# A gated unit moved into an attention loop, a third bank for its scores, and an output projection taken up group by group

## The chip, the cores and the metric

The kernel runs on one core of one Trainium2 chip. The metric is the device time of one execution in microseconds; of three executions of the kernel before the median is 3381.57 us.

The engines are named as the profile names them: PE is the matrix engine (TensorE), ACT the scalar engine, DVE the vector engine, POOL GpSimd, SP the engine that issues most transfers. Each works through its own list of instructions in order and stops at a semaphore that is not there yet.

## What is computed

Two layers, each with a mixer, a cross-attention to a memory, and a large expert stage. The change lies in the mixer alone. Cut to what matters, the mixer is:

```python
c_q, c_kv, k_r, u_ssm, q_sb, k_sb, v_sb = split_columns(x @ w_in, IN_WIDTHS)
y_mla = chunk_causal_softmax_attention(q, k, v)        # latent attention, 6 heads of 64
y = jax.nn.gelu(scan_of(u_ssm))                        # state space part, 384 wide
y_ssm = y * jax.nn.sigmoid(y @ w_glu + b_glu)          # the gated unit
y_sb = stick_breaking_attention(q_sb, k_sb, v_sb)      # 4 heads of 64
y = jnp.concatenate([group_rms(y_mla), group_rms(y_ssm), group_rms(y_sb)], axis=-1) * g_mix
mix = y @ w_out                                        # the output projection, 1024 x 1024
```

The sequence has 512 positions, the model is 1024 wide. The program approximates gelu by tanh both before and after the change.

## The kernel before, in words

Everything is held transposed: features on the 128 partitions, the 512 positions along the free axis. y has eight such tiles: 0 to 2 are the latent attention, 3 to 5 the state space part (they lie in u), 6 and 7 the stick-breaking attention. The order of every engine is written out by hand in the function mixer, with one inner function per engine; semaphores tie them together. Nothing reorders it.

**The loop of the latent attention.** It has 24 turns, i = 0 to 23: six heads with four query blocks each (block b = i mod 4 sees b + 1 blocks of 128 keys). A turn's work goes round four stations. PE makes the scores (mla_s, line 898, one matmul 128 to 512 wide), DVE takes their largest value (mla_max), ACT takes the exponential into prob (line 1107), DVE scales it by the sum (mla_scale), PE transposes it, one 128x128 matrix per key block (mla_t, line 907), ACT copies the result out of PSUM into probT (mla_copy, line 1525), and PE multiplies it with the values (mla_o, line 921). prob and probT have two slots each, and the scores two banks, 4 and 5. Two waits matter below. ACT's exponential of turn i writes the slot that the transposes of i - 2 read, so it waits for them:

```python
            if i >= 2:
                act.wait_ge(m.mla_tr, i - 1)
```

And mla_o(i) waits until ACT has copied turn i (`pe.wait_ge(m.mla_pt, i + 1)`). In program turn i, PE issues mla_s(i + 1), mla_t(i - 1), mla_o(i - 2); ACT issues the exponential of i, then the copy of i - 2, and after the last block of every second head one copy of the result (mla_out, line 1531).

Into the first twelve turns DVE has the last two units of the state space scan strewn, six pieces each; PE has ssm_in and ssm_out for them (lines 829, 844, 847). After ssm_skip(2) on DVE, SP sends the scan's result out to DRAM and back in another layout, into u.

**The tail.** After the loop ACT squares y tiles 6, 7, 0, 1, 2 (line 1121), PE sums the squares over the partitions with a matrix of ones (squares, line 951), and ACT makes 1/rms of the two attention groups with a Ln and an Exp (rms, lines 1127 and 1129). ACT loads the table for gelu, applies it to u (line 1144), and loads the one for sigmoid. PE makes the nine products of the gated unit (line 960), ACT the sigmoid (line 1151), DVE the product, then come the squares and the rms of the third group. Each y tile is scaled (norm, line 1463), split into a high half in 16 bits by ACT (high, line 1133) and the rest by DVE (low, line 1471), for the matmuls take three 16-bit products in place of one in 32 bits. The state space tiles are read and written with a stride there (in_time).

**The output projection** has eight tiles of 128 output features. Each tile takes 8 x 3 = 24 matmuls 512 wide (project, lines 127 to 129). Tiles 0 and 1 are begun with the five y tiles of the attention groups and finished with the last three, tiles 2 to 7 follow, in two banks by turns. Weight tiles come through a ring of four (RING): DMA into wf, high half by ACT, low by DVE, then used; a slot is free when tile_used counts its last use. Behind the projection PE goes on with the memory's key tiles (256 wide, the first at line 127 with work as its input), the layer norm's sums between them.

## Time and profile before

| | us |
|---|---|
| median of three executions | 3381.57 (3372.29, 3381.57, 9482.11) |
| the profiled execution | 3381.33 |
| its span, first to last instruction | 3379.6 |
| PE busy in the span | 3208.7 (95%) |
| DVE, ACT busy | 2717.6, 1411.2 |
| layer 1: first score of the loop to last transposes | 176.59 to 227.90 |
| layer 1: last transposes to the end of the output projection | 227.90 to 297.51 |
| layer 2: the same end points | 1907.82 and 1978.86 |

Times within an execution are microseconds from the first instruction. The clock column of the stage table is PE's granted clock as a share of 2.4 GHz: 0.50 is the lower of its two levels, 1.2 GHz. A row of the time line gives the start, the duration, and, in brackets, how long the engine had stood idle and what released it. Durations of neighbouring rows on PE overlap, since matmuls are pipelined: the step from one start to the next is the price in a full stream. A matmul in 32 bits appears as two.

### The profile page before, as it was taken

The numbers are of one execution on the slowest core, as the hardware profiler recorded it, in microseconds if no ns is written. First come the engines' busy times: TensorE is split into PE (matmuls) and PEld (weight loads), VectorE is DVE, ScalarE is ACT, GpSimd is POOL, SyncE is SP. The second block draws the span as 40 slices with busy tenths as digits, with TensorE's granted clock in tenths as the row PEclk, the third lists the DMA queues.
The fourth block names the chain that finished last, engine by engine and source line by source line (L and its number), as shares of the span: only waits on it lengthen the run. The fifth ranks groups of instructions, "written<-read, shape, count | busy, mean of one in ns | idle before, by whom it ended". The sixth has DMA issues, their size and how long they took to land. (4 is left out here: it accounts for less than half of the span.)

```text
span 3379.6 us, 58399 instructions
## 1 busy us (share of the span) xinstructions
PE 3208.7 (95%) x20362; PEld 1966.0 (58%) x20362; DVE 2717.6 (80%) x5214; ACT 1411.2 (42%) x2117; POOL 1005.3 (30%) x754
## 2 busy tenths in 40 slices
PE   7989999999999899999799899999999998999996
PEld 3645665565666566666445465655656665666663
DVE  6866458898999788888877563688989997888887
ACT  4454443343444333333444543433444443333333
POOL 2400000332404344444324000003424144444442
PEclk9999999999999999999899999999999999999998
DMA  5103222889898999999551032338898989999994
GB/s 195 48 13 106 94 94 96 293 279 365 277 340 288 402 389 386 397 397 366 192 161 35 13 131 69 107 101 301 271 379 278 329 302 403 388 386 399 390 371 181
DMA packets 395484, 846.02 MB, mean 250 GB/s; under 512 B 34368, under 2 KB 239168, under 8 KB 394560
## 3 DMA queue, kind: packets, MB, share of 16 engines
q1 hardware_dynamic: 321024, 570.38, 47.6%
q0 software_dynamic: 73728, 268.47, 22.2%
q10 hardware_dynamic: 576, 5.37, 0.4%
q8 instruction: 64, 1.05, 0.1%
q14 instruction: 92, 0.75, 0.1%
HBM read 733.99 MB, written 110.10 MB: 250 GB/s over the span
## 5 line engine op out<-in xcount | busy, mean ns | idle before, releaser
L98 ACT ACTIVATE wh<-wf 128x1024 f16<-128x1024 f32 x656 | 690.8, 1053 | 947.9 <-PE ps L2132 545.8
L127 PE MATMUL ps<-xh,wh 128*128 128x384 f16 (+2 forms) x3008 | 1011.7, 336 | 78.2 <-DVEq L1273 37.4
L129 PE MATMUL ps<-xh,wl 128*128 128x384 f16 (+2 forms) x3008 | 1011.1, 336 | 0.0
L128 PE MATMUL ps<-xl,wh 128*128 128x384 f16 (+2 forms) x3008 | 1010.9, 336 | 0.0
L104 DVE SCALAR_TENSOR_TENSOR wl<-wf,wh 128x1024 f16<-128x1024 f32 x656 | 801.4, 1222 | 222.0 <-ACT wh L98 203.5
L2130 PE MATMUL ps<-work,wh 128*128 128x384 f16 x2048 | 668.9, 327 | 8.0 <-DVE work L2462 6.1
L2132 PE MATMUL ps<-work,wl 128*128 128x384 f16 x2048 | 669.2, 327 | 0.0
L2131 PE MATMUL ps<-work,wh 128*128 128x384 f16 x2048 | 669.1, 327 | 0.0
L2247 POOL DMA_INDIRECT xT<-urows,small x256 | 390.4, 1525 | 904.9 <-DVE xT L2330 650.4
L2256 POOL DMA_INDIRECT work<-experts,small x256 | 451.0, 1762 | 559.7 <-DVE work L2471 533.7
L127 PEld LDWEIGHTS ps<-xh,wh 128*128 128x128 f16 x3008 | 296.3, 99 | 303.3 <-DVEq L1273 38.4
L129 PEld LDWEIGHTS ps<-xh,wl 128*128 128x128 f16 x3008 | 296.1, 98 | 222.3 <-issue 5.3
L128 PEld LDWEIGHTS ps<-xl,wh 128*128 128x128 f16 x3008 | 296.2, 98 | 212.1 <-issue 6.4
L2471 DVE SCALAR_TENSOR_TENSOR work<-work,small 128x1024 f32<-128x1024 f32 x256 | 328.7, 1284 | 97.2 <-DVE work L2462 96.5
L2330 DVE SCALAR_TENSOR_TENSOR xT<-xT,work 128x1024 f32<-128x1024 f32 x256 | 308.2, 1219 | 72.6 <-DMA xT<-urows,small 71.6
L2130 PEld LDWEIGHTS ps<-work,wh 128*128 128x128 f16 x2048 | 200.8, 98 | 141.8 <-issue 8.0
L2132 PEld LDWEIGHTS ps<-work,wl 128*128 128x128 f16 x2048 | 200.7, 98 | 133.0 <-issue 1.0
L2131 PEld LDWEIGHTS ps<-work,wh 128*128 128x128 f16 x2048 | 200.8, 98 | 132.2 <-issue 1.3
L2189 ACT ACTIVATE work<-ps 128x384 f32<-128x384 f32 x192 | 93.7, 488 | 334.5 <-PE ps L129 334.4
L2457 DVE TENSOR_TENSOR work<-work 128x384 f32<-128x384 f32 x256 | 141.0, 551 | 0.5 <-DMA work<-gates 0.5
L2462 DVE SCALAR_TENSOR_TENSOR work<-work 128x384 f16<-128x384 f32 x256 | 141.0, 551 | 0.0
L220 POOL TENSOR_SCALAR xT<-xT,small 128x512 f32<-128x512 f32 x16 | 27.2, 1701 | 368.7 <-ACT xh L199 368.7
(414 smaller groups left out, 3746.7 us busy)
## 6 DMA issues: line engine op xcount, KB each, us to landing
wf<-experts SPq DMA_DIRECT2D x512, 512.0 KB, 6.9
wf<-proj SPq DMA_DIRECT2D x144, 512.0 KB, 3.4
gates<-work SPq DMA_DIRECT2D x96, 512.0 KB, 8.1
work<-hid SPq DMA_DIRECT2D x256, 192.0 KB, 4.8
work<-gates SPq DMA_DIRECT2D x256, 192.0 KB, 6.3
hid<-work SPq DMA_DIRECT2D x192, 192.0 KB, 5.3
hid<-small SPq DMA_DIRECT2D x64, 192.0 KB, 5.3
xsave<-xT ACTq DMA_DIRECT2D x2, 2048.0 KB, 6.5
```

The source lines that it names most:

```text
L98: m.nc.scalar.activation(m.wh[:, slot, :], m.wf[:, k, :], ACT.Copy, scale=WS).then_inc(m.high_done, 1)
L104: m.nc.vector.scalar_tensor_tensor(m.wl[:, slot, :], m.wf[:, k, :], WS, m.wh[:, slot, :], ALU.mult, ALU.subtract).then_inc(m.split_done, 1)
L127: m.nc.tensor.matmul(out, wh[:, k, :], xh[:, k, 0:n], start=(k == order[0]), stop=False)
L128: m.nc.tensor.matmul(out, wh[:, k, :], xl[:, k, 0:n], start=False, stop=False)
L129: last = m.nc.tensor.matmul(out, wl[:, k, :], xh[:, k, 0:n], start=False, stop=(k == order[-1]))
L2130: MM(out, m.wh[:, k, c], ph[:, k, :], start=first, stop=False)
L2131: MM(out, m.wh[:, k, c], pl[:, k, :], start=False, stop=False)
L2132: done = MM(out, m.wl[:, k, c], ph[:, k, :], start=False, stop=last)
L2247: pool.indirect_dma_start(urow[:, i % GR, :], None, a.urows, bass.IndirectOffsetOnAxis(ap=uidx[:, i:i + 1], axis=0))\
L2256: pool.indirect_dma_start(vrow[:, i % GR, :], None, rows, bass.IndirectOffsetOnAxis(ap=vidx[:, i:i + 1], axis=0))\
L2330: STT(row, row, 1.0, xtok, ALU.mult, ALU.mult, accum_out=hd[:, i:i + 1]).then_inc(m.dots, 1)
L2471: STT(acc, row, wd[:, bass.ds(i, 1)], acc, ALU.mult, ALU.add).then_inc(m.added, 1)
```

## The change

- **Scores run two turns ahead.** mla_s(i + 2) stands where mla_s(i + 1) stood, in three banks (4, 5, 1). ssm_in of the units from 4 on keeps to bank 0 and waits for one more unit.
- **mla_o(i - 2) is issued before mla_t(i - 1).** Before, it was the other way round.
- **The gated unit goes into the loop.** gelu and sigmoid are written with tanh: ACT squares u, DVE makes u(1 + c u^2), ACT takes the tanh, DVE makes (tanh + 1) u, twice gelu; the sigmoid likewise is half of 1 + tanh of half its argument. The factor 4 that this leaves is taken back by SSM_PART = 0.25. Turns 15 to 18 hold the gelu, turns 18 to 23 the nine products on PE, turns 18 to 20 four squares, turns 21, 22 and the end the gate. One table set holds Exp, Tanh, Square and Copy; it is loaded once ahead of the loop, and the one for Ln behind it. Before, three were loaded in the tail.
- **The output projection goes group by group.** Four tiles in four banks take up y tiles 6 and 7, then 3, 4, 5, then 0, 1, 2; then tiles 4 to 7 follow whole. The sums of four squares are made right behind the last transposes, the other four behind the first part.
- ssm_skip(2) comes one turn earlier (13).

```diff
+Y_ORDER = [6, 7, 3, 4, 5, 0, 1, 2]
+SSM_TILES = (3, 4, 5)
+SSM_PART = 0.25
+SQUARES = [(6, 1, 0, 2), (7, 1, 1, 2), (0, 0, 0, 3), (1, 0, 1, 3), (3, 2, 0, 3), (4, 2, 1, 3), (5, 2, 2, 3), (2, 0, 2, 3)]
+GROUP_BANK = {1: (4, 0), 0: (5, 1), 2: (1, 2)}
+GLU_I = 15
+GLU_AT = {18: ((0, 0), (0, 1)), 19: ((1, 0), (1, 1)), 20: ((0, 2),), 21: ((1, 2),), 22: ((2, 0), (2, 1)), 23: ((2, 2),)}
+GELU_CUBE = 0.044715
+GELU_SCALE = (2 / math.pi) ** 0.5
+EXP_TANH = "exp_and_others"
...
+    def score_bank(i):
+
+        return B[(4, 5, 1)[i % 3]]
+
+    def glu_bank(j):
+
+        return B[(0, 2)[j % 2]]
+
+    def out_bank(f):
+
+        return B[(0, 2, 3, 6)[f % RING]]
...
-            if i >= 2:
-                pe.wait_ge(m.mla_e, i - 1)
+            if i >= 3:
+                pe.wait_ge(m.mla_e, i - 2)
             n = P * (b + 1)
-            MM(B[4 + i % 2][:, 0:n], qh[:, h, b * P:n], kh[:, h, 0:n], start=True, stop=True)\
+            MM(score_bank(i)[:, 0:n], qh[:, h, b * P:n], kh[:, h, 0:n], start=True, stop=True)\
...
+        def glu_product(j, c):
+            if (j, c) == (0, 0):
+                pe.wait_ge(m.glu_in, 16)
+            if j == 0:
+                pe.wait_ge(m.gelu_done, (3, 4, 6)[c])
+            if (j, c) == (2, 0):
+                pe.wait_ge(m.glu_sig, 7)
+            last = MM(glu_bank(j), glu[:, c, j * P:(j + 1) * P], u[:, c, :], start=(c == 0), stop=(c == 2))
+            if c == 2:
+                last.then_inc(m.glu_mm, 1)
+
         for i in range(len(iters)):
-            if i and i + 1 < len(iters):
-                mla_s(i + 1)
+            if i + 2 < len(iters):
+                mla_s(i + 2)
             if i % PIECES == 0 and i and BH + i // PIECES - 1 < UNITS:
                 ssm_out(BH + i // PIECES - 1)
             if i == 1:
                 pe.wait_ge(m.ssm_y, 2)
+            if i >= 2:
+                mla_o(i - 2)
             if i >= 1:
                 mla_t(i - 1)
-            if i >= 2:
-                mla_o(i - 2)
...
+            for j, c in GLU_AT.get(i, ()):
+                glu_product(j, c)
         mla_t(len(iters) - 1)
+
+        def squares(i):
+            g, c, n = SQUARES[i][1:]
+            if c == 0:
+                pe.wait_ge(m.mla_e, len(iters) - 2 + GROUP_BANK[g][1])
+            pe.wait_ge(m.grp_sq, i + 1)
+            MM(B[GROUP_BANK[g][0]], m.ones[:, :], sqs[:, i % 4, :], start=(c == 0), stop=(c == n - 1))\
+                .then_inc(m.grp_sum, 1)
+
+        for i in range(4):
+            squares(i)
         mla_o(len(iters) - 2)
         mla_o(len(iters) - 1)
 
-        def squares(i, g, c, n):
-            pe.wait_ge(m.grp_sq, i + 1)
-            MM(B[4 + g], m.ones[:, :], sqs[:, i % 4, :], start=(c == 0), stop=(c == n - 1))\
-                .then_inc(m.grp_sum, 1)
-
-        for i, x in enumerate([(1, c, 2) for c in range(2)] + [(0, c, 3) for c in range(3)]):
-            squares(i, *x)
-        pe.wait_ge(m.glu_in, 16)
-        pe.wait_ge(m.gelu_done, 3)
-        for j in range(3):
...
-        for c in range(3):
-            squares(5 + c, 2, c, 3)
-        order = [6, 7, 0, 1, 2, 3, 4, 5]
-        pe.wait_ge(m.yl_done, 5)
-        pe.wait_ge(m.glu_sig, 3)
-        for f in range(2):
+        def projected_part(k0, k1):
+            pe.wait_ge(m.yl_done, k1)
+            for f in range(RING):
+                n = N_IN + f
+                if k0 == 0:
+                    wait_tile(m, pe, n // RING, n % RING)
+                last = project(m, out_bank(f), n % RING, m.xh, m.xl, SEQ, Y_ORDER, slice(k0, k1))
+                if k1 == KT:
+                    last.then_inc(m.tile_used, 1)
+
+        pe.wait_ge(m.glu_sig, 9)
+        pe.wait_ge(m.mla_pt, len(iters))
+        projected_part(0, 2)
+        for i in range(4, KT):
+            squares(i)
+        projected_part(2, 5)
+        projected_part(5, KT)
+        for f in range(RING, N_OUT):
             n = N_IN + f
             wait_tile(m, pe, n // RING, n % RING)
...
+            pe.wait_ge(m.ln_mix.res_added, f - RING + 1)
+            project(m, out_bank(f), n % RING, m.xh, m.xl, SEQ).then_inc(m.tile_used, 1)
...
+        def glu_square(j):
+            act.wait_ge(m.ssm_y, GROUPS)
+            act.wait_ge(m.moved_back, 16 * STRIDE * (GROUPS + j + 1))
+            AF(sig[:, j, :], u[:, j, :], ACT.Square, scale=GELU_CUBE ** 0.5).then_inc(m.glu_sig, 1)
+
+        def glu_tanh(j):
+            act.wait_ge(m.gelu_done, (1, 2, 5)[j])
+            AF(sig[:, j, :], sig[:, j, :], ACT.Tanh, scale=GELU_SCALE).then_inc(m.glu_sig, 1)
+
+        def glu_gate(j):
+            act.wait_ge(m.glu_mm, j + 1)
+            AF(sig[:, j, :], glu_bank(j), ACT.Tanh, scale=0.25, bias=half_glu[:, j:j + 1]).then_inc(m.glu_sig, 1)
+
+        def square(i):
+            f = SQUARES[i][0]
+            if i >= 4:
+                act.wait_ge(m.grp_sum, i - 3)
+            AF(sqs[:, i % 4, :], y[f], ACT.Square, scale=SSM_PART if f in SSM_TILES else 1.0).then_inc(m.grp_sq, 1)
+
+        act.preload_act_table_set(EXP_TANH)
...
+            if i == GLU_I:
+                glu_square(0)
+                glu_square(1)
+            if i == GLU_I + 1:
+                glu_tanh(0)
+                glu_tanh(1)
+            if i == GLU_I + 2:
+                glu_square(2)
+            if i == GLU_I + 3:
+                glu_tanh(2)
+                act.wait_ge(m.sb_y, 2)
+                square(0)
+            if i == GLU_I + 4:
+                square(1)
+                act.wait_ge(m.mla_y, 2)
+                square(2)
+            if i == GLU_I + 5:
+                square(3)
+            if i == GLU_I + 6:
+                glu_gate(0)
+            if i == GLU_I + 7:
+                glu_gate(1)
         mla_copy(m, act, len(iters) - 2, iters, probT, B)
         mla_copy(m, act, len(iters) - 1, iters, probT, B)
-        mla_out(m, act, len(iters) - 1, iters, y, B)
...
+        glu_gate(2)
+        act.preload_act_table_set(LOG_EXP)
...
+        rms(0, 1, 2, BH * BD)
+        mla_out(m, act, len(iters) - 1, iters, y, B)
+        act.wait_ge(m.tile_used, N_IN + RING)
+        for i in range(2):
+            high(i)
+        for i in range(4, 7):
+            act.wait_ge(m.gelu_done, i + 3)
+            square(i)
         act.wait_ge(m.mla_y, 3)
-        for i in range(5):
-            square(i)
-        rms(0, 1, 2, BH * BD)
-        rms(1, 0, 5, MH * MV)
-        act.preload_act_table(ACT.Gelu_apprx_tanh)
-        for j in range(3):
-            act.wait_ge(m.moved_back, 16 * STRIDE * (GROUPS + j + 1))
...
-        for j in range(3):
...
+        def gelu_argument(j):
+            dve.wait_ge(m.glu_sig, (1, 2, 5)[j])
+            STT(sig[:, j, :], sig[:, j, :], 1.0, u[:, j, :], ALU.add, ALU.mult).then_inc(m.gelu_done, 1)
+
+        def gelu_twice(j):
+            dve.wait_ge(m.glu_sig, (3, 4, 6)[j])
+            STT(u[:, j, :], sig[:, j, :], 1.0, u[:, j, :], ALU.add, ALU.mult).then_inc(m.gelu_done, 1)
+
+        def gated(j):
+            dve.wait_ge(m.glu_sig, 7 + j)
+            dve.wait_ge(m.glu_mm, 3)
+            STT(u[:, j, :], sig[:, j, :], 1.0, u[:, j, :], ALU.add, ALU.mult).then_inc(m.gelu_done, 1)
+
+        TS(half_glu, par[:, PAR["b_glu"]], 0.5, None, ALU.mult)
         for i in range(len(iters)):
             mla_max(i)
             if i == 1:
@@ -1438,8 +1521,18 @@
                 mla_scale(i - 1)
             n, piece = BH + i // PIECES, i % PIECES
             if n >= UNITS:
-                if (n, piece) == (UNITS, 2):
+                if (n, piece) == (UNITS, 1):
                     ssm_skip(2)
+                if i == GLU_I:
+                    gelu_argument(0)
+                    gelu_argument(1)
+                if i == GLU_I + 1:
+                    gelu_twice(0)
+                    gelu_twice(1)
+                if i == GLU_I + 2:
+                    gelu_argument(2)
+                if i == GLU_I + 3:
+                    gelu_twice(2)
...
+        for j in range(3):
+            gated(j)
         norm(1, 1, (0, 1))
-        norm(0, 2, (2, 3, 4))
-        for i in range(5):
+        for i in range(2):
             low(i)
-        for j in range(3):
-            dve.wait_ge(m.glu_sig, j + 1)
-            dve.wait_ge(m.glu_mm, 3)
-            TT(u[:, j, :], u[:, j, :], sig[:, j, :], ALU.mult).then_inc(m.glu_done, 1)
-        dve.wait_ge(m.grp_sq, 8)
-        norm(2, 3, (5, 6, 7))
+        norm(2, 2, (2, 3, 4))
+        for i in range(2, 5):
+            low(i)
+        norm(0, 3, (5, 6, 7))
...
```

The order on PE within a turn, before (scores are line 898, transposes 907, products with the values 921). These are program turns 8 and 9: scores of 9, transposes of 7, products of 6, then scores of 10, transposes of 8, products of 7:

```order
L898 MATMUL ps<-work 128x256 [waits mla_e]
L907 MATMUL ps<-ident,work 128x128 [waits mla_pt,mla_p]
L907 MATMUL ps<-ident,work 128x128 x3
L921 MATMUL ps<-work 64x128 [waits mla_pt]
L921 MATMUL ps<-work 64x128 x2
L898 MATMUL ps<-work 128x384 [waits mla_e]
L907 MATMUL ps<-ident,work 128x128 [waits mla_pt,mla_p]
L921 MATMUL ps<-work 64x128 [waits mla_pt]
L921 MATMUL ps<-work 64x128 x3
```

And now, program turns 7 and 8 (scores are line 925, transposes 934, products with the values 948): scores of 9, products of 5, transposes of 6, then scores of 10, products of 6, transposes of 7:

```order
L925 MATMUL ps<-work 128x256 [waits mla_e]
L948 MATMUL ps<-work 64x128 [waits mla_pt]
L948 MATMUL ps<-work 64x128
L934 MATMUL ps<-ident,work 128x128 [waits mla_pt,mla_p]
L934 MATMUL ps<-ident,work 128x128 x2
L925 MATMUL ps<-work 128x384 [waits mla_e]
L948 MATMUL ps<-work 64x128 [waits mla_pt]
L948 MATMUL ps<-work 64x128 x2
L934 MATMUL ps<-ident,work 128x128 [waits mla_pt,mla_p]
L934 MATMUL ps<-ident,work 128x128 x3
```

The products with the values now stand behind the scores and ahead of the transposes; before, the transposes stood between.

The end of the loop on PE before (951 the sums of squares, 960 the gated unit, 127 the projection):

```order
L921 MATMUL ps<-work 64x128 [waits mla_pt]
L921 MATMUL ps<-work 64x128 x3
L951 MATMUL ps<-work,ones 128x512 [waits grp_sq] x5
L960 MATMUL ps<-work 128x512 [waits gelu_done,glu_in]
L960 MATMUL ps<-work 128x512 x8
L951 MATMUL ps<-work,ones 128x512 [waits grp_sq] x3
L127 MATMUL ps<-xh,wh 128x512 [waits split_done,glu_sig,yl_done]
L128 MATMUL ps<-xl,wh 128x512
```

And now (966 the gated unit, 992 the sums of squares):

```order
L966 MATMUL ps<-work 128x512
L934 MATMUL ps<-ident,work 128x128 [waits mla_pt,mla_p]
L934 MATMUL ps<-ident,work 128x128 x3
L992 MATMUL ps<-work,ones 128x512 [waits grp_sq,mla_e]
L992 MATMUL ps<-work,ones 128x512 [waits grp_sq]
L992 MATMUL ps<-work,ones 128x512 [waits grp_sq,mla_e]
L992 MATMUL ps<-work,ones 128x512 [waits grp_sq]
L948 MATMUL ps<-work 64x128 [waits mla_pt]
L948 MATMUL ps<-work 64x128 x2
L948 MATMUL ps<-work 64x128 [waits mla_pt]
L948 MATMUL ps<-work 64x128 x3
L127 MATMUL ps<-xh,wh 128x512 [waits yl_done,split_done,mla_pt,glu_sig]
```

The nine products are gone from this place, four sums stand ahead of the last products with the values, and the projection follows at once, with its waits.

ACT in turns 15 to 17 now (1169 the exponential, 1617 the copy, 1145 the square and 1149 the tanh of the gelu):

```order
L1169 ACTIVATE work,small<-ps,small 128x512 [waits mla_tr,mla_nm]
L1617 ACTIVATE work<-ps 128x256 [waits mla_av,mla_tr]
L1145 ACTIVATE sq<-work 128x512 [waits moved_back,ssm_y] x2
L1169 ACTIVATE work,small<-ps,small 128x128 [waits mla_tr,mla_nm]
L1617 ACTIVATE work<-ps 128x384 [waits mla_av,mla_tr]
L1149 ACTIVATE sq<-sq 128x512 [waits gelu_done] x2
L1169 ACTIVATE work,small<-ps,small 128x256 [waits mla_tr,mla_nm]
L1617 ACTIVATE work<-ps 128x512 [waits mla_av,mla_tr]
L1145 ACTIVATE sq<-work 128x512 [waits moved_back,ssm_y]
L1169 ACTIVATE work,small<-ps,small 128x384 [waits mla_tr,mla_nm]
```

The tanh of turn 16 waits for DVE, which waits for the square of turn 15; neither was in the loop before.

## Rows read from the trace of the kernel before

**Rows 1.** Busy time by stage: length, busy us of each engine, PE's clock, DMA.

```profile
170.00:176.00 6.00, 3.36 (x19) 2.17 (x18) 4.17 (x10) 1.24 (x1) 3.21 (x5) 1.00 0.00 0
242.00:244.00 2.00, 2.00 (x4) 0.68 (x3) 1.36 (x3) 2.00 (x4) 0.00 (x0) 0.50 0.00 0
```

**Rows 2.** Time line of PE, one head of the loop, layer 1.

```profile
211.56 0.55 PE L907 MATMUL ps<-ident,work 128*128 128x128 f32 x3 [0.50 <-DVE work L1431]
...
212.70 0.70 PE L898 MATMUL ps<-work 128*128 128x256 f32 x2
213.24 0.60 PE L907 MATMUL ps<-ident,work 128*128 128x128 f32 x4
...
214.57 0.91 PE L898 MATMUL ps<-work 128*128 128x384 f32 x2
215.31 0.27 PE L907 MATMUL ps<-ident,work 128*128 128x128 f32 x1
...
216.53 1.12 PE L898 MATMUL ps<-work 128*128 128x512 f32 x2
217.50 0.38 PE L907 MATMUL ps<-ident,work 128*128 128x128 f32 x2
...
218.17 0.49 PE L898 MATMUL ps<-work 128*128 128x128 f32 x2
```

**Rows 3.** Time line of PE, program turns 5 and 6 of layer 1.

```profile
190.36 1.09 PE L921 MATMUL ps<-work 128*64 128x128 f32 x8 [0.36 <-ACT work L1525]
191.38 1.12 PE L898 MATMUL ps<-work 128*128 128x512 f32 x2
...
193.68 0.38 PE L907 MATMUL ps<-ident,work 128*128 128x128 f32 x2
```

**Rows 4.** Time line of ACT, turns 2 to 7 of layer 1.

```profile
183.26 0.58 ACT L1107 ACTIVATE work<-ps,small 128x384 f32<-128x384 f32 x1 [2.31 <-DVE small L1425]
...
189.26 0.48 ACT L1107 ACTIVATE work<-ps,small 128x256 f32<-128x256 f32 x1 [1.60 <-DVE small L1425]
...
189.72 0.59 ACT L1525 ACTIVATE work<-ps 128x512 f32<-128x512 f32 x1
...
194.16 0.69 ACT L1107 ACTIVATE work<-ps,small 128x512 f32<-128x512 f32 x1 [2.34 <-PE ps L907]
```

**Rows 5.** Time line of PE, the tail of layer 1.

```profile
227.90 0.66 PE L907 MATMUL ps<-ident,work 128*128 128x128 f32 x4
...
231.74 4.56 PE L951 MATMUL ps<-work,ones 128*128 128x512 f32 x10 [1.41 <-ACT work L1121]
240.81 9.66 PE L960 MATMUL ps<-work 128*128 128x512 f32 x18 [4.51 <-ACT work L1144]
253.18 2.84 PE L951 MATMUL ps<-work,ones 128*128 128x512 f32 x6 [2.72 <-ACT work L1121]
255.86 0.38 PE L127 MATMUL ps<-xh,wh 128*128 128x512 f16 x1
```

**Rows 6.** Time line of PE, where the memory's tiles begin, layer 1.

```profile
297.51 0.27 PE L127 MATMUL ps<-work,wh 128*128 128x256 f16 x1
```

**Rows 7.** Time line of PE, the last three squares of layer 2.

```profile
1933.00 4.36 PE L951 MATMUL ps<-work,ones 128*128 128x512 f32 x6 [2.72 <-ACT work L1121]
```

**Rows 8.** Time line of ACT, the tail of layer 1.

```profile
240.68 1.28 ACT L1145 ACT_TABLE_LOAD   x1
241.97 2.71 ACT L1133 ACTIVATE xh<-work 128x512 f16<-128x512 f32 x5
...
256.06 0.69 ACT L1127 ACTIVATE work<-ps,eps 128x512 f32<-128x512 f32 x1 [1.90 <-PE ps L951]
...
258.31 3.09 ACT L1133 ACTIVATE xh<-work 128x512 f16<-128x512 f32 x3 [0.90 <-DVE work L1463]
```

**Rows 9.** Time line of DVE, the tail of layer 1.

```profile
257.53 2.08 DVE L1463 SCALAR_TENSOR_TENSOR work<-work,small 128x512 f32<-128x512 f32 x3 [5.06 <-ACT work L1129]
259.52 2.96 DVE L1471 SCALAR_TENSOR_TENSOR xl<-work,xh 128x512 f16<-128x512 f32 x3
```

More of the change, by code:

```diff
@@ L668, in mixer @@
     mx, nmx, rsum, rinv = (small.take([2]) for _ in range(4))
+    half_glu = small.take([3])
     y = [qh[:, 2 * j, :] for j in range(3)] + [u[:, j, :] for j in range(3)] + [qsb[:, j, :] for j in range(2)]
@@ L828, in ssm_in @@
                     st = 2 * n + i
-                    last = MM(cols(B[n % 2], 2 * z + i), in_weights(z, st), inputs_of(st), start=True, stop=True)
+                    last = MM(cols(in_bank(n), 2 * z + i), in_weights(z, st), inputs_of(st), start=True, stop=True)
             last.then_inc(m.ssm_bu, 1)
@@ L958, in tensor @@
-        for j in range(3):
-            for c in range(3):
-                last = MM(B[j], glu[:, c, j * P:(j + 1) * P], u[:, c, :], start=(c == 0), stop=(c == 2))
-            last.then_inc(m.glu_mm, 1)
-        for c in range(3):
-            squares(5 + c, 2, c, 3)
-        order = [6, 7, 0, 1, 2, 3, 4, 5]
-        pe.wait_ge(m.yl_done, 5)
-        pe.wait_ge(m.glu_sig, 3)
-        for f in range(2):
+        def projected_part(k0, k1):
[7 more added lines that the diff above has]
+                    last.then_inc(m.tile_used, 1)
@@ L968, in tensor @@
+        pe.wait_ge(m.glu_sig, 9)
[6 more added lines that the diff above has]
+        for f in range(RING, N_OUT):
             n = N_IN + f
             wait_tile(m, pe, n // RING, n % RING)
-            project(m, B[f], n % RING, m.xh, m.xl, SEQ, order, slice(0, 5))
-        pe.wait_ge(m.yl_done, KT)
-        for f in range(2):
-            project(m, B[f], (N_IN + f) % RING, m.xh, m.xl, SEQ, order, slice(5, KT))\
-                .then_inc(m.tile_used, 1)
@@ L1106, in scalar @@
                 act.wait_ge(m.sb_o, BH)
-            AF(prob[:, i % 2, 0:n], B[4 + i % 2][:, 0:n], ACT.Exp, scale=MLA_SCALE,
+            AF(prob[:, i % 2, 0:n], score_bank(i)[:, 0:n], ACT.Exp, scale=MLA_SCALE,
                bias=nmx[:, i % 2:i % 2 + 1], accum_out=rsum[:, i % 2:i % 2 + 1]).then_inc(m.mla_e, 1)
@@ L1131, in high @@
         def high(i):
+            f = Y_ORDER[i]
             act.wait_ge(m.y_norm, i + 1)
-            AF(*in_time(m.xh[:, order[i], :], y[order[i]], i >= 5), ACT.Copy, scale=XS).then_inc(m.yh_done, 1)
-        act.wait_ge(m.sb_y, 2)
-        act.wait_ge(m.mla_y, 3)
-        for i in range(5):
-            square(i)
-        rms(0, 1, 2, BH * BD)
-        rms(1, 0, 5, MH * MV)
-        act.preload_act_table(ACT.Gelu_apprx_tanh)
-        for j in range(3):
-            act.wait_ge(m.moved_back, 16 * STRIDE * (GROUPS + j + 1))
-            AF(u[:, j, :], u[:, j, :], ACT.Gelu_apprx_tanh).then_inc(m.gelu_done, 1)
-        act.preload_act_table(ACT.Sigmoid)
-        act.wait_ge(m.tile_used, N_IN + RING)
-        for i in range(5):
-            high(i)
-        for j in range(3):
-            act.wait_ge(m.glu_mm, j + 1)
-            AF(sig[:, j, :], B[j], ACT.Sigmoid, bias=par[:, PAR["b_glu"]][:, j:j + 1]).then_inc(m.glu_sig, 1)
-        act.preload_act_table_set(LOG_EXP)
-        for j in range(3):
-            act.wait_ge(m.glu_done, j + 1)
-            square(5 + j)
-        rms(2, 2, 8, SG * SC)
-        for i in range(5, KT):
+            AF(*in_time(m.xh[:, f, :], y[f], f in SSM_TILES), ACT.Copy,
+               scale=XS * SSM_PART if f in SSM_TILES else XS).then_inc(m.yh_done, 1)
+        rms(0, 1, 2, BH * BD)
[6 more added lines that the diff above has]
+            square(i)
+        act.wait_ge(m.mla_y, 3)
+        square(7)
+        rms(1, 2, 7, SG * SC)
+        rms(2, 0, 8, MH * MV)
+        for i in range(2, KT):
             high(i)
@@ L1421, in mla_max @@
             dve.wait_ge(m.mla_sc, i + 1)
-            step(nc.vector.reduce_max(mx[:, k:k + 1], B[4 + k][:, 0:n], AX.X))
+            step(nc.vector.reduce_max(mx[:, k:k + 1], score_bank(i)[:, 0:n], AX.X))
             if i >= 2:
@@ L1455, in vector @@
         mla_scale(len(iters) - 1)
-        order = [6, 7, 0, 1, 2, 3, 4, 5]
         def norm(k, need, tiles):
@@ L1461, in norm @@
             for i in tiles:
-                f = order[i]
+                f = Y_ORDER[i]
                 STT(y[f], y[f], par[:, PAR["g_mix"]][:, f:f + 1], grs[:, k, :], ALU.mult, ALU.mult)\
```

39 lines of the change are left out of this document (14 added, 25 removed).

## The prediction, made before the change was run

> **What bounds the kernel now.** I read the profile from the outside in. The page first: PE, the matrix engine, is busy for 95% of the span, and nearly all the rest of the program, the experts above all, is untouched. Whatever the change does, it does in the mixer of each layer, between the first score of the latent attention and the end of the output projection, two stretches of some 121 us. PE's time line comes next, for PE is the engine that starts the following stage, and everything behind the mixer hangs on its data: a microsecond won or lost there goes through to the end at face value. What counts is therefore PE's idle time and PE's clock in the two stretches.
>
> In the loop, the time line of one head shows PE nearly full. From the start of a turn's transposes to the next scores, transposes and products with the values take 1.14, 1.33, 1.22 and 0.67 us, together **4.36** a head; the scores take 0.54, 0.74 and 0.97 for 256, 384 and 512 columns, by the same spacing 0.33 for 128, together 2.58 [rows 2]. PE is thus busy 6.94 us a head, and the only pause of that head is 0.50.
>
> In the tail, from the last transposes at 227.90 to the memory's first tile at 297.51, 69.6 us pass in layer 1. PE pauses 1.41, 4.51 and 2.72 us there [rows 5, 6]. After the pause of 4.51 the granted clock is 0.50 [rows 1], and the nine products of the gated unit take 9.66 us. Five squares of the same width take 4.56 at full clock, 0.88 each without the overlap at the end, so nine cost 7.9 and the low clock costs **1.7**. After the pause of 2.72 the three squares take 2.84 in layer 1 and 4.36 in layer 2 [rows 5, 7]: there the clock fell in one of two cases. Layer 2's tail is 71.1 by that.
>
> **The loop: the order of transposes and values.** This is the part on which my forecast rests. ACT's exponential of turn i waits for the transposes of i - 2, then ACT copies these transposes out, then PE can make the products of i - 2. Before, PE had the transposes of i - 1 to issue between, so ACT worked while PE did. Now the products of i - 2 stand ahead of the transposes of i - 1. Only the scores of i + 2 cover ACT's two instructions, and the next transposes, which the next exponential waits for, come after. PE and ACT take turns in a ring: exponential, copy, values, transposes, exponential.
>
> ACT's share: exponentials of 256 and 512 columns take 0.48 and 0.69, one of 384 takes 0.58, so 0.37 for 128 and 2.12 for four. The copy of 512 takes 0.59; with the same steps four take 1.72. The handover is 0.05 from the copy's end (189.72 + 0.59) to PE's start at 190.36, and from PE to ACT 0.10 (193.68 + 0.38 to 194.16) plus about 0.07 of the transposes' tail that runs beyond their step: 0.2 a turn [rows 3, 4]. A head is 2.12 + 1.72 + 0.8 + 4.36 = **9.0 us**, where PE's own work is 6.94.
>
> Two ahead instead of one helps the scores, which then are never late, but they were not what held a full PE. I start where DVE still sets the pace in both versions, at the exponential of turn 2 at 183.26 [rows 4]. Turns 2 and 3 take 1.7 + 2.4, five heads 45.0, less the first handover: 48.9. ssm_out comes twice, 1.34 each (191.38 + 0.97 to 193.68) [rows 3]; what of it is not covered by the gap in the ring is 0.6 and 1.0. The last transposes would start at 183.26 + 50.5 = 233.8 instead of 227.90: **+5.9**.
>
> The other moves in the loop: ssm_in a turn later and in one bank costs nothing, since DVE has read the unit before long before and the gap in the ring hides it. The table load ahead of the loop, 1.28 [rows 8], delays the first exponential, hidden behind DVE's scan and skip work; uncovered it would be 1.3. ssm_skip one turn earlier is 0.
>
> **The gated unit in the loop.** Nine products at full clock: 7.9. Those in turns 18 to 23 fill gaps in the ring, 0.3 or 0.7 a turn, 3.2 in all. Against that stands a chain between ACT and DVE in turns 15 to 18. In turn 15 the two arguments on DVE wait for ACT's square (0.6) and take 0.7 each [rows 9]; the largest value of turn 16 (0.4 with its scaling) is queued behind them, so its exponential starts 2.4 after the copy of turn 13 and not 1.3: 1.1 lost. The same way I get 0.9 in turn 17, 0.5 in 18 and 0.7 in 19 with ACT's tanh, square and result copy in front: 3.2. Bounds: 0, if DVE runs far enough ahead, to 6, twice as much, if each of the four waits also holds the turn behind it. I take 3.2; with the filled gaps it cancels, and the unit costs **7.9**. The DMA of the scan's result has four turns, 9 us, before it is needed, and costs 0. The loop thus ends 5.9 + 7.9 = **13.8 us later**.
>
> **The tail now.** PE: last transposes 0.6, four squares 3.5, two products with values 1.8 = 5.9. ACT meanwhile: copy 0.6, gate 0.7, table 1.28, Ln and Exp 0.7 each, done before PE is. Then a result copy 0.6, two high halves 0.6 each, the last low half 0.7: PE starts the first part at 8.4, after a **pause of 2.5**. A matmul of the projection is (297.51 - 255.86) / 192 = 0.217 [rows 5, 6]. First part, 24 of them: 5.2. Four squares: 3.5, PE free at 17.1. The third of them, at 16.2, releases Ln and Exp of the state space group, Ln and Exp of the latent group stand behind on ACT (2.8 in all), then three strided high halves, 3.09, then the last strided low half, 1.0 [rows 8, 9]: 23.1, a **pause of 6.0**. Then 72 matmuls 15.6 and four whole tiles 20.8: 59.5. The weight tiles of the ring come free 1.9 us apart instead of 5.2, but the first is needed 5.9 after its slot is free, and ACT and DVE need about 3 for it: 0.
>
> The clock: the pause of 6.0 is longer than the 4.51 that cost 1.7, so 1.7 again. The pause of 2.5 is nearest to the 2.72 that cost 0 and 1.5: I take 0.8, ends 0 and 1.5. Tail 62.0, against 69.6 and 71.1: **7.6 and 9.1 won**.
>
> A switch of ACT's table: its load ends at 241.96 and the next ACTIVATE starts at 241.97 [rows 8]; nothing stands between. The Trainium skill (ScalarE: Activation LUTs, What ACT_TABLE_LOAD costs) adds a drain to each load, about 2.66 us for the switch; by that, ACT would finish in the tail at about the time of PE's last products, and the sum would be 0.2 us higher. I go by the row.
>
> **The sum.** 13.8 - 7.6 = 6.2 in layer 1, 13.8 - 9.1 = 4.7 in layer 2: 10.9, say 11. The profiled execution took 3381.3 (span 3379.6, 1.7 around it), which is also the median shown: **3392**. The nine products are moved, not removed; what the tail wins is mostly their time.
>
> **Rivals.**
> - *The ring has slack, the scores two ahead do their work.* Then the copy is not what ends last, PE runs at 6.94 a head, and the loop loses its pauses, like the 0.50 at transposes that waited for DVE [rows 2]; I put eight such as gone, 4 us. Loop -4 + 7.9 + 3.2 = +7.1, less 7.6 and 9.1: -2.5, so 3379; without the chain's 3.2, 3372. For it: the scores are early. Against it: the waits in the code leave no way round. 17%.
> - *The chain and the clock cost their upper bounds.* Another 3 us for the gelu and 0.7 for the clock in each layer: 3400; with DVE late for whole turns, 3405. 10%.
> - *Slower beyond doubt: the clock falls in the loop.* With a pause in every turn PE's busy share there drops from 0.93 to about 0.77. If the clock went to its lower level for the whole loop, a head would take 4.4 more plus scores no longer covered, and the nine products 7.9 more, some 43 us a layer: 3480. For half the loop, 3435. It decides where short pauses alone are enough. Against it: a stage of 6 us with PE busy for 3.36 has clock 1.00 [rows 1]. The Trainium skill (TensorE: Matmul & The Clock Gate, A second HAM failure mode) tells of a kernel that cycled through PSUM banks and, with small pauses between its groups, lost its clock again and again; that is this rival. 3%, half of it over 2%.
> - *It does not do what it says.* Nothing reorders the lists, and ACT's holds two table loads where three were. I give it nothing.
>
> **Chances and range.** The forecast's own case has 70%: 3384 to 3400. The 17% of slack spread from 3372 to 3383. The range leaves out its lower third and the top: **3375 to 3402**. 2% of the time is 68 us, about what a measurement of this kernel tells from no change; only the clock reaches it. Faster 0.01, same 0.97, slower 0.02.
>
> **What would show it.** In the profile after, a head of the loop in turns 4 to 15 takes 9.0 us, PE's idle time in the loop is ended by ACT's copy (before: by DVE), and ACT's idle time ahead of the exponential by PE's transposes. The last transposes of layer 1 start near 242. The nine products take 0.9 each. In the tail, pauses of about 2.5 and 6, the low clock after the second. The forecast is wrong if PE does not wait for the copy in the loop, or if the loop's last transposes start before 238.

## The result, and the profile after

The changed kernel takes **3389.29 us** (3387.14 to 3389.84, 5 runs), the kernel before 3380.96 (3372.29 to 9482.11, 5 runs); the ratio is 1.0034, 95% interval 1.0019 to 1.0048. One slow run of the kernel before, of 9482.11 us, is left out of the ratio. In a second comparison, with 12 and 17 runs, the ratio was 1.0040 (1.0027 to 1.0052). By the two ratios it is slower by 11.5 and 13.5 us; the medians differ by 8.3 and 15.0. The prediction said +11 and 3392, with a range of 3375 to 3402.

Stages of both layers, from the profiled executions (loop: exponential of turn 2 to the start of the last transposes; tail: from there to the memory's first tile; mixer part: first transposes to the memory's first tile):

| us | loop 1 | tail 1 | mixer part 1 | loop 2 | tail 2 | mixer part 2 |
|---|---|---|---|---|---|---|
| before | 44.64 | 69.61 | 115.59 | 44.65 | 71.04 | 117.02 |
| predicted | 58.4 | 62.0 | | 58.4 | 62.0 | |
| after | 58.39 | 63.46 | 123.19 | 61.26 | 61.77 | 124.36 |
| after, second profile | 58.39 | 63.46 | 123.18 | 58.38 | 63.47 | 123.19 |

PE's time line in the loop after, turns 7 to 9 of layer 1 (948 values, 934 transposes, 925 scores), answers to [rows 2]:

```profile
196.59 0.65 PE L948 MATMUL ps<-work 128*64 128x128 f32 x4 [0.77 <-ACT work L1617]
197.18 0.55 PE L934 MATMUL ps<-ident,work 128*128 128x128 f32 x3
197.56 0.81 PE L925 MATMUL ps<-work 128*128 128x384 f32 x2
198.71 0.87 PE L948 MATMUL ps<-work 128*64 128x128 f32 x6 [0.34 <-ACT work L1617]
199.51 0.66 PE L934 MATMUL ps<-ident,work 128*128 128x128 f32 x4
200.00 1.02 PE L925 MATMUL ps<-work 128*128 128x512 f32 x2
201.37 1.09 PE L948 MATMUL ps<-work 128*64 128x128 f32 x8 [0.34 <-ACT work L1617]
```

In these turns every group of products with the values has a pause in front that ACT's copy ends (where state space work or a product of the gated unit stands in between, there is none); before, one pause in a head stood in front of the transposes and was DVE's. ACT's time line of the same place (1169 exponential, 1617 copy), answering to [rows 4]:

```profile
197.82 0.37 ACT L1169 ACTIVATE work<-ps,small 128x128 f32<-128x128 f32 x1 [1.28 <-PE ps L934]
...
198.18 0.48 ACT L1617 ACTIVATE work<-ps 128x384 f32<-128x384 f32 x1
...
202.82 0.58 ACT L1169 ACTIVATE work<-ps,small 128x384 f32<-128x384 f32 x1 [1.50 <-PE ps L934]
...
203.39 0.27 ACT L1617 ACTIVATE work<-ps 128x128 f32<-128x128 f32 x1
```

Each exponential begins when PE's transposes are done, the copy follows at once, and ACT then stands idle until the next transposes. The two engines take turns. Without state space work or a result copy, the steps between the starts of PE's products are 2.12 and 2.66 (196.59, 198.71, 201.37) and, a head later, 2.33 and 2.01 (211.97, 214.30, 216.31): 9.12 us a head put together from the two, for 9.0 forecast. The product of turn 12 is the row of 214.30; it is used again below:

```profile
214.30 0.43 PE L948 MATMUL ps<-work 128*64 128x128 f32 x2 [0.77 <-ACT work L1617]
```

Who ended PE's idle time in the whole loop of layer 1, after and then before (total, times, longest):

```profile
PE ps L948 <- ACT work L1617: 9.0, 12, 1.7
PE ps L948 <- ACT work L1623: 3.1, 2, 1.8
```

```profile
PE ps L907 <- DVE work L1431: 3.4, 5, 0.9
PE ps L921 <- ACT work L1525: 0.4, 1, 0.4
```

In turns 15 to 18 the pauses are longer. DVE (1504 argument, 1491 largest value, 1494 its scaling, 1508 twice the gelu) and ACT (1145 square, 1169 exponential):

```profile
216.80 1.29 DVE L1504 SCALAR_TENSOR_TENSOR sq<-sq,work 128x512 f32<-128x512 f32 x2 [2.07 <-ACT sq L1145]
218.01 0.28 DVE L1491 TENSOR_REDUCE small<-ps 128x1 f32<-128x128 f32 x1
218.33 0.15 DVE L1494 TENSOR_SCALAR small<-small 128x1 f32<-128x1 f32 x1
...
219.91 1.29 DVE L1508 SCALAR_TENSOR_TENSOR work<-sq,work 128x512 f32<-128x512 f32 x2 [0.83 <-ACT sq L1149]
```

```profile
216.14 1.15 ACT L1145 ACTIVATE sq<-work 128x512 f32<-128x512 f32 x2
218.52 0.37 ACT L1169 ACTIVATE work<-ps,small 128x128 f32<-128x128 f32 x1 [1.23 <-DVE small L1494]
...
221.76 0.47 ACT L1169 ACTIVATE work<-ps,small 128x256 f32<-128x256 f32 x1 [1.36 <-DVE small L1494]
```

DVE stands idle 2.07 us for ACT's square, with the largest value of turn 16 queued behind, and the exponential of turn 16 waits for that; the same once more in turn 17.

PE's tail after, answering to [rows 5, 6] (992 squares, 127 projection, work,wh the memory's tile):

```profile
242.38 0.60 PE L934 MATMUL ps<-ident,work 128*128 128x128 f32 x4
242.82 3.60 PE L992 MATMUL ps<-work,ones 128*128 128x512 f32 x8
246.35 1.74 PE L948 MATMUL ps<-work 128*64 128x128 f32 x14
```

```profile
250.83 0.38 PE L127 MATMUL ps<-xh,wh 128*128 128x512 f16 x1 [2.74 <-DVE xl L1563]
...
257.69 3.60 PE L992 MATMUL ps<-work,ones 128*128 128x512 f32 x8
267.08 0.61 PE L127 MATMUL ps<-xh,wh 128*128 128x512 f16 x1 [5.79 <-DVE xl L1563]
...
305.84 0.27 PE L127 MATMUL ps<-work,wh 128*128 128x256 f16 x1
```

Pauses of 2.74 and 5.79 us, for 2.5 and 6.0 forecast. The clock (columns: window, length, busy time and count of PE, weight loads, DVE, ACT and POOL, the granted clock, DMA share, GB/s; the windows are the first part, the second part, and two places in the loop of layer 2):

```profile
252.00:258.00 6.00, 6.00 (x21) 2.50 (x20) 0.00 (x0) 0.00 (x0) 0.00 (x0) 0.74 0.01 3
266.00:268.00 2.00, 0.92 (x3) 0.37 (x4) 2.00 (x4) 0.28 (x1) 0.00 (x0) 0.50 0.00 0
270.00:272.00 2.00, 2.00 (x6) 0.76 (x5) 0.81 (x2) 0.00 (x0) 0.00 (x0) 0.50 0.00 0
...
1866.00:1870.00 4.00, 3.51 (x15) 2.84 (x15) 3.83 (x14) 1.49 (x6) 0.00 (x0) 0.57 0.24 70
1910.50:1914.00 3.50, 3.50 (x8) 1.50 (x7) 2.38 (x9) 2.09 (x5) 0.00 (x0) 0.51 0.02 5
```

After the first pause the clock is low for part of the stage at 252. Around the second it is at 0.50 from 265.3 to 272.1, 6.8 us of which PE works 5.1; after the pause of 4.51 before, it was low for 3.4 us. And it fell twice in the loop of layer 2, which explains 61.26 there against 58.39.

### The profile page after: what moved, and what is told of

The parts are those of the page before. It is cut to its first block and busy times, and to the rows that moved or that the text cites. A ratio compares the mean times of both kernels' runs of the same rounds, so it can differ in the third digit from the quotient of the medians.

```text
span 3385.4 us, 58423 instructions
## 1 busy us (share of the span) xinstructions
PE 3202.6 (95%) x20362; PEld 1962.7 (58%) x20362; DVE 2726.4 (81%) x5228; ACT 1412.8 (42%) x2121; POOL 996.5 (29%) x754
## 5 line engine op out<-in xcount | busy, mean ns | idle before, releaser
L2422 DVE SCALAR_TENSOR_TENSOR xT<-xT,work 128x1024 f32<-128x1024 f32 x256 | 308.7, 1222 | 60.4 <-DMA xT<-urows,small 59.5
```

Source lines behind the costliest of these rows:

```text
L2422: STT(row, row, 1.0, xtok, ALU.mult, ALU.mult, accum_out=hd[:, i:i + 1]).then_inc(m.dots, 1)
```

## The experiments

Every comparison shares one chip with runs of the kernel before. Times of the whole spread over some 14 us from run to run (the kernel before: 3371.31 to 3384.95 in the 29 runs of one comparison), the mixers' stages repeat within 0.02 us from profile to profile unless the clock differs; so the stages decide, and the whole is a check.

**The kernel before, again** (no edit).

> The kernel before, once more, for a second profile of it. It tells how far the same program drifts between two executions in the stages that the change does not touch. Theory A (the change costs about 19 us in the two mixers, and the stages between and behind them, which stream the experts' weights, came out about 13 us shorter in the profiled run of the changed kernel by chance): the mixers last as before within 0.5 us (layer 1 from the first transposes of the loop to the memory's first tile 115.6 us, layer 2 117.0), while the stretch from layer 1's mixer to layer 2's differs by several us from the 1564 us of before. Theory B (the shorter expert stages are an effect of the change): that stretch comes out as before within 1 us.

Mixer parts 115.61 and 117.03: the same. The stretch from layer 1's mixer to layer 2's took 1564.6 (first profile 1564.3), the rest behind 1400.9 (1400.7). Theory A's second half failed, B's held in this pair. In the ten profiles of the other kernels the stretch between the mixers took 1558.4 to 1562.2. More on it below.

**Transposes first.**

```diff
-            if i >= 2:
-                mla_o(i - 2)
             if i >= 1:
                 mla_t(i - 1)
+            if i >= 2:
+                mla_o(i - 2)
```

> The changed kernel with one pair of lines swapped back: the transposes of turn i - 1 are issued ahead of the products with the values of turn i - 2. Theory A (the ring between PE and ACT costs 5.9 us a layer): layer 1 from the exponential of turn 2 to the last transposes falls from 58.4 us to 52.5, a head without state space work takes 7.0 to 7.3 us and not 9.1, the whole 12 us less than the changed kernel, 3377. Rival (the gelu chain or DVE holds the loop anyway): the loop falls by less than 2 us, the whole by less than 4.

Loop 52.98 and 52.99, whole 3376.51 (ratio to before 1.000, 0.999 to 1.001). One pair of lines takes **5.4 us** from each loop and 12.1 us from the two mixer parts together (116.92 and 117.32); by the ratios, 1.0034 and 1.0040 against 1.000, it is 11 to 14 us of the whole. A head took 7.56 (transposes at 194.96 and 202.52), with a result copy and one pause for DVE in it, a little over the 7.0 to 7.3 expected. PE's waits in the loop of layer 1 are now:

```profile
PE ps L934 <- DVE work L1500: 4.4, 5, 1.3
PE ps L948 <- ACT work L1623: 0.5, 1, 0.5
PE ps L948 <- ACT work L1617: 0.4, 1, 0.4
```

The copy is gone from the list but for 0.4; DVE is back, 4.4. Of that, 2.7 (1.29, 0.53 and 0.85) stand in turns 16 to 18, and the other 1.7 in turns 2 and 11.

**The kernel before, values first.**

```diff
-            if i >= 1:
-                mla_t(i - 1)
             if i >= 2:
                 mla_o(i - 2)
+            if i >= 1:
+                mla_t(i - 1)
```

> The kernel before with only that pair of lines swapped: the products with the values of turn i - 2 ahead of the transposes of turn i - 1; scores stay one turn ahead. Theory A: the ring appears here too, a head takes 9.0 us and not 7.6, layer 1 from the exponential of turn 2 to the last transposes grows from 44.6 us to 50.5, the whole by 12 us to about 3390. Rival (the ring needs the scores two ahead, or the gated unit in the loop, to show): less than 2 us in the loop.

Loops 55.16 and 54.11, whole 3397.51 (ratio 1.0053, 1.0035 to 1.0071). The waits and the clock, of the loop of layer 1 and of 3.4 us in it:

```profile
PE ps L921 <- ACT work L1525: 10.8, 15, 1.2
PE ps L921 <- ACT work L1531: 1.4, 2, 0.7
```

```profile
183.00:237.00 54.00, 41.41 (x221) 26.86 (x220) 33.11 (x111) 21.50 (x68) 0.00 (x0) 0.94 0.05 16
206.60:210.00 3.40, 3.40 (x16) 3.21 (x14) 0.94 (x4) 0.84 (x3) 0.00 (x0) 0.51 0.00 0
```

The ring is there without gated unit and without scores further ahead. The loops grew by 10.5 and 9.5 us. The clock fell twice in the first loop and once in the second. Each fall can be priced by the same steps at full clock: 4.48 between the products of turns 9 and 10 where the changed kernel takes 3.05, so 1.4, and 2.75 and 3.07 late in the loop for 2.12 and 2.66, so 1.0. That leaves 8.1 us in both layers for the ring, where I had said 5.9. Rows of layer 2, at full clock, show where the miss lies (the row x7 holds the last seven transposes; the last four of them, where the loop ends, start at 1926.72):

```profile
1904.97 0.43 PE L921 MATMUL ps<-work 128*64 128x128 f32 x2
...
1911.75 1.09 PE L921 MATMUL ps<-work 128*64 128x128 f32 x8 [0.55 <-ACT work L1525]
1914.66 0.40 PE L921 MATMUL ps<-work 128*64 128x128 f32 x2 [0.71 <-ACT work L1531]
...
1926.34 0.98 PE L907 MATMUL ps<-ident,work 128*128 128x128 f32 x7
```

A turn whose copy is followed by a result copy (L1531) takes 2.91 and not 2.33: 0.6, twice, which the forecast of the ring left out. The first ssm_out costs 0.5 more than assumed, and a head 9.12 for 9.0, 0.6 over five heads.

**The kernel before, scores two ahead.**

```diff
-            if i and i + 1 < len(iters):
-                mla_s(i + 1)
+            if i + 2 < len(iters):
+                mla_s(i + 2)
```

with the banks (4, 5, 1) for the scores, bank 0 for the state space inputs, and ssm_in a turn later.

> The kernel before with only the scores two turns ahead in three banks (and, as that needs, the state space inputs in one bank, a turn later); transposes stay ahead of the products with the values. Theory A (scores ahead take away PE's waits for DVE): the pauses in the loop fall from 5.3 us to about 1.5, layer 1 from the exponential of turn 2 to the last transposes from 44.6 us to 41, the whole by 7 us. Rival (DVE sets the pace in the first half, so only the second half gains): 43, the whole 3 us less.

Loops 41.30 and 41.30, whole 3368.06 (ratio 0.9970, 0.9959 to 0.9981): 3.3 us a loop, and 7.5 in the medians of the whole. This part of the change, alone, makes the kernel faster. PE's waits in the loop:

```profile
PE ps L907 <- DVE work L1431: 1.7, 2, 1.3
PE ps L921 <- ACT work L1525: 0.4, 1, 0.4
```

**Filling the pauses of the tail.**

```diff
+        pe.wait_ge(m.mla_e, len(iters))
+        for _ in range(3):
+            MM(B[1][:, 0:3 * P], m.ones[:, :], glu[:, 0, :], start=True, stop=True)
         pe.wait_ge(m.glu_sig, 9)
...
         for i in range(4, KT):
             squares(i)
+        for _ in range(6):
+            MM(B[7], m.ones[:, :], sqs[:, 0, :], start=True, stop=True)
         projected_part(2, 5)
```

> The changed kernel with matmuls that compute nothing wanted put into PE's two pauses of the tail: three of 384 columns ahead of the projection's first part, six of 512 behind the last squares, the results unused. Theory A (the low clock after the pauses costs the projection 1.6 us and 2.9 us in layer 1, 2.9 us in layer 2): the clock stays at 1.00 to the end of the projection, the tail of layer 1 falls from 63.5 us to about 59.5, that of layer 2 from 61.8 to 59, the whole by 6 us. Rival (what costs is the pause, and its clock is repaid by the filling matmuls being late): the tail falls by less than 1 us or grows.

Tail 59.32 in both layers, whole 3381.22 (ratio 1.0011, 1.0001 to 1.0021). PE (1012 and 1019 are the filling):

```profile
251.13 2.20 PE L1012 MATMUL ps<-work,ones 128*128 128x384 f32 x6
253.93 0.38 PE L127 MATMUL ps<-xh,wh 128*128 128x512 f16 x1 [0.60 <-DVE xl L1568]
...
262.54 5.31 PE L1019 MATMUL ps<-work,ones 128*128 128x512 f32 x12
268.54 0.39 PE L127 MATMUL ps<-xh,wh 128*128 128x512 f16 x1 [0.69 <-DVE xl L1568]
```

The projection's parts begin 8.4 and 23.1 us behind the last transposes, as late as without filling in layer 2 of the first profile, where the first part ran at full clock; all of it now runs at full clock. The tail's low clock had cost 63.46 - 59.32 = **4.1 us** in layer 1, and 61.77 - 59.32 = 2.45 in layer 2, where only the second pause brought it. So it costs 1.65 behind the first pause and 2.45 behind the second; the 2.9 of my expectation is too high. The loop of layer 1 took 60.89 here, with the clock low in it for 6.8 us; that of layer 2 58.37.

**Two tiles instead of four, group by group.**

```diff
-            for f in range(RING):
+            for f in range(2):
...
-        for f in range(RING, N_OUT):
+        for f in range(2, N_OUT):
...
-            pe.wait_ge(m.ln_mix.res_added, f - RING + 1)
+            if f >= RING:
+                pe.wait_ge(m.ln_mix.res_added, f - RING + 1)
```

> The changed kernel with two tiles instead of four in the group by group part of the projection; tiles 2 to 7 follow whole, in the same four banks. Theory A (the pauses are set by ACT's and DVE's chain from the squares on, and four tiles only move that chain 2.6 us later): the first part takes 2.6 us less, the squares and all behind them come 2.6 us earlier, and the six tiles that follow take as much longer; tail of layer 1 63.5 us within 1, the whole the same within 3. Rival (four tiles cover what two leave open): a third pause of 1 to 3 us appears ahead of the last part, and the whole grows by 2 to 6 us.

Tails 63.17 and 63.01, loops 58.39 and 58.40, whole 3386.26 (ratio 1.0029, 1.0019 to 1.0040). Two tiles do as well as four: what is put ahead of the squares delays the chain behind them by as much.

**Transposes first, gelu spread, high halves earlier.** In DVE's list the parts of the gelu stand in turns 16 to 19 instead of 15 to 18; in the tail:

```diff
         rms(1, 2, 7, SG * SC)
+        for i in range(2, 5):
+            high(i)
         rms(2, 0, 8, MH * MV)
-        for i in range(2, KT):
+        for i in range(5, KT):
             high(i)
```

> The kernel with the transposes first again (3376.5), and two orders changed besides: DVE's part of the gelu one turn later in its list, so that it finds ACT's result ready, and in the tail the high halves of the state space tiles ahead of the Ln and Exp of the latent group. Theory A (the chain between ACT and DVE costs about 3 us in the loop, the order of Ln and Exp 1.3 in the tail): layer 1's loop falls from 53.0 us to 50, its tail from 62.6 to 61.3, the whole by 8 us to about 3368. Rival (the loop is held by something else, such as ACT's full list in turns 15 to 22): the loop falls by less than 1 us.

Loops 49.13 and 49.12, whole 3369.85 (ratio 0.9975, 0.9964 to 0.9985). The spread takes **3.85 us** from the loop. PE's waits there:

```profile
PE ps L934 <- DVE work L1502: 1.7, 2, 1.3
PE ps L948 <- ACT work L1625: 0.5, 1, 0.5
```

The tail did not move: 62.83 and 63.12 against 62.60 and 62.99. The pause fell from 5.79 to 5.52 only. ACT shows why:

```profile
255.00 0.63 ACT L1206 ACTIVATE work<-work 128x512 f32<-128x512 f32 x1
256.45 3.04 ACT L1211 ACTIVATE xh<-work 128x512 f16<-128x512 f32 x3 [0.82 <-DVE work L1557]
```

The high halves now wait 0.82 for DVE's scaling, which before went on beside the second Ln and Exp. My 1.3 had left that out.

**All together, with filling** (three and four matmuls).

> All together: transposes first, DVE's gelu a turn later, high halves ahead of the second Ln and Exp, and filling matmuls in both pauses (three of 384 columns, four of 512, results unused). Theory A: first transposes to the memory's first tile 109 us in both layers, where the kernel before takes 115.6 and 117.0 and the one with only the scores two ahead 113.7 and 112.3; the whole 14 us below before, 3362. Rival (the filling matmuls delay real work as much as the clock gives back): no better than without them.

Mixer parts 109.51 and 109.49; whole **3362.64** (ratio 0.9954, 0.9937 to 0.9971). It beats both kernels, by 15 us the one before.

**The changed kernel again** (no edit).

> The changed kernel once more, for a second profile and for a comparison on one chip with more runs. Theory A (the loop's clock falls now and then, since PE pauses in every turn): the loop of each layer takes 58.4 us, or up to 3 more where the clock falls in it; the two mixers together cost 13 to 17 us more than before (14.9 in the first profile); the whole 3388, 0.3 to 0.4% over before. Rival (the first profile's 61.3 us in layer 2 has another cause): both loops differ from 58.4 with the clock at 1.00 throughout.

Loops 58.39 and 58.38 with the clock at 1.00 in both, whole 3391.14 (ratio 1.0040). Mixer parts 13.8 us over before.

**Scores two ahead, with filling.** To the kernel with only the scores ahead:

```diff
         pe.wait_ge(m.glu_in, 16)
+        for _ in range(6):
+            MM(B[3][:, 0:3 * P], m.ones[:, :], glu[:, 0, :], start=True, stop=True)
         pe.wait_ge(m.gelu_done, 3)
...
+        for _ in range(3):
+            MM(B[3][:, 0:3 * P], m.ones[:, :], glu[:, 0, :], start=True, stop=True)
         for c in range(3):
             squares(5 + c, 2, c, 3)
```

> The kernel before with the scores two turns ahead, and filling matmuls of 384 columns in two pauses of its tail (six ahead of the gated unit's products, three ahead of the last squares, results unused). Theory A (the low clock costs this kernel 1.7 us at the products, and sometimes as much at the squares): the tail of both layers takes 67.9 us in place of 71.1 and 69.6, first transposes to the memory's first tile 110.5, the whole 5 us less than without the filling, 3363; the gated unit in the loop (109.5 with everything else mended) is then worth 1 us a layer. Rival (the moved gated unit is worth more): this kernel stays 3 us a layer or more behind it.

Tail 67.85 in both layers, mixer parts 110.49, whole 3362.89 (ratio 0.9953, 0.9935 to 0.9972). The nine products, 9.66 in [rows 5], at full clock:

```profile
240.44 7.99 PE L962 MATMUL ps<-work 128*128 128x512 f32 x18 [0.55 <-ACT work L1148]
```

Against 109.5 of the kernel with everything mended, the gated unit in the loop and the projection by groups are worth 1.0 us a layer by the stages. The whole does not tell the two apart (3362.64 and 3362.89, the intervals nearly the same).

## Why the prediction was right, point by point

**The loop.** Forecast +13.8, measured +13.75 in layer 1. The experiments take it apart; they nest, each differing from the next by one thing, but for the third line, where the gated unit and the tail's new form are added together:

| | loop, us | step | forecast |
|---|---|---|---|
| before | 44.64 | | |
| scores two ahead | 41.30 | -3.3 | to 41.3, PE's own work |
| gated unit, no waits in its chain | 49.13 | +7.8 | +7.9 |
| the chain between ACT and DVE | 52.98 | +3.85 | +3.2 |
| values ahead of transposes | 58.39 | +5.4 | +6.0 |

The forecast column is worked out of the prediction. Its loop without the gated unit was 50.5 long. The ring's gaps, 9.0 less 6.94 or 2.06 a head, are some 10.3 in the five heads; 1.1 of ssm_out's 2.7 was to lie in them, so the ring adds 9.2, and 41.3 are left for PE's own work. Products were to fill 3.2 of the gaps, so beside the gated unit the ring costs 6.0. The one step that made the forecast, that mla_o ahead of mla_t turns PE and ACT into a ring, is shown: by the waits after, by undoing it, and by doing it alone.

That the sum came out within 0.1 us was luck: two terms missed by about 1.5 us, one each way. No run has the ring with the scores two ahead and without the gated unit, but rows give an estimate of it. The changed kernel reaches the product of turn 12, still ahead of the gated unit, 30.3 us after the exponential of turn 2 (183.99 to 214.30). From there to the last transposes the kernel before with the values first takes 21.75 at full clock (1904.97 to 1926.72). Together that is a loop of some 52.1, so the ring costs some 7.4 where I had 5.9, for the reasons given at that run, and the gated unit some 6.3 where I had 7.9. By the same estimate the gaps are 10.8 and not 9.2, and the products fill some 5.4 of them and not 3.2 (10.8 less 5.4); the chain took 3.85 and not 3.2.

**The clock in the loop.** I gave it 3% as a rival with large prices, and nothing in the forecast. It does happen, rarely and at a small price: in the ten loops profiled with the values first it fell in four, and the loop grew by 2.5 (60.89 against 58.37) and 2.9 (61.26 against 58.38) where the same kernel's undisturbed loop stands beside it; in the 14 loops with the transposes first, never. One stage of 6 us at full clock with PE busy for 3.36 of it [rows 1] was too little evidence for a loop of 60.

**The tail.** Pauses 2.74 and 5.79 for 2.5 and 6.0; the chain of ACT and DVE was sized right. Without its clock the tail is 59.3 us (59.32 with filling), for 59.5 forecast. The clock was mis-sized: 1.65 and 2.45 us in layer 1 where I took 0.8 and 1.7. I had taken the cost of the pause of 4.51 for the longer one too, but PE worked at the low clock for 5.1 us after it, not 3.4. 62.0 became 63.46. That the group by group part wins nothing by having four tiles the prediction did not say, though its sum (59.5 whatever stands ahead of the squares) held it.

**The whole.** "Goes through to the end at face value" is not shown. In the first pair of profiles the mixers grew by 14.9 us and the span by 5.8; the stretches between and behind were 5.9 and 4.0 shorter. One piece of that is seen: both profiles of the kernel before have the clock low for 3.4 us in the layer norm behind the first mixer (at 306.0 and 307.6), those of the changed kernel have not. The rest lies in the expert stages. Between the mixers the clock records of the traces are low for 54.6 us in both profiles of the kernel before and for 44.4 in both of the changed kernel; PE's work at half speed for 10.2 us less would be up to 5.1 us, an estimate, of the 5.9 and of 5.0 in the second pair. What makes the clock differ there is not shown, and it is not all: with the values first alone it was low for 54.6 us too, and that stretch took 1562.2. By the ratios the whole grew by 11.5 and 13.5, near the mixers' 14.9 and 13.8; the profiled executions of the kernel before (3381.3, 3383.2) lie above most of its medians (3380.96, 3375.61, 3377.00 and 3376.17), those of the changed one (3387.14 and 3384.18) below its own (3389.29 and 3391.14). Whether more than such scatter is in it stays open. My +11 met the whole partly for this reason; the mixers alone were mis-sized by 3 to 4. In the second profile all of its 2.9 is the clock in the two tails, 1.5 in each; in the first the clock in the loop of layer 2 adds 2.9, and the tail there is 1.7 shorter.

**The rivals.** Slack in the ring is refuted. The chain at its upper bound is refuted: 3.85. The large price of the clock is refuted for the ten loops seen. That the scores ahead do work of their own is half borne out: alone they take 3.3 us from a loop, but in the ring some 0.7 is left of it (8.1 less the estimated 7.4).

## What to carry to other kernels

When two engines hand slots to each other, look at what one can still issue between the instruction the other waits for and the one that waits for it: one swapped pair of lines cost 5.4 us in 24 turns and hid a gain of 3.3 beside it. Work moved into a full loop costs its own length there, and pays only by what it frees at its old place, here 1 us a layer. Pauses of a few microseconds can be paid twice, once as idle time and once as a slower clock behind them: in the ten unfilled tails of the changed kernel and its variants the clock was low behind the longer pause (5.5 to 5.8 us) every time and behind the shorter (2.7) nine times. And a forecast that meets the number can still have two terms wrong: compare it stage by stage.

## What the runs showed that I had not expected

- Matmuls that compute nothing, put into pauses of 2.7 and 5.8 us, won 4.1 us of 63.5 in the changed tail of layer 1, and made both layers' tails equal to 0.01 us; without them the same tail varied from 61.77 to 63.47.
- The clock also differs from execution to execution ahead of the loop, where nothing was changed (from 135 to 182 us its mean was 1.00 in one profile of the changed kernel and 0.93 in the other): the first transposes start at 181.4 to 188.9 us in the twelve profiles. The latest is that of the two tiles, where the granted clock from 135 to 182 us was 0.85 in the mean; in the earliest it was 1.00.
